# Two 4 MB loads in place of four 2 MB loads for each expert's gate-up weights

## The reference, cut to what matters

```
logits = t @ router_w + router_b                 # 1024 tokens, 32 experts
top_logit, top_idx = top_k(logits, 4); gates = softmax(top_logit)
for each expert e, for the tokens that chose it:
    gu   = t[tok] @ w_gate_up[e] + b_gate_up[e]  # (n, 1024) @ (1024, 2048), gate and up columns alternate
    gate = minimum(gu[:, 0::2], 7); up = clip(gu[:, 1::2], -7, 7)
    act  = (up + 1) * gate * sigmoid(1.702 * gate)
    y    = act @ w_down[e] + b_down[e]           # (n, 1024) @ (1024, 1024)
out[token] = x[token] + sum of gate * y over the token's 4 experts
```

## Time and profile before

| | us |
|---|---|
| median of 3 runs | 3649.79 |
| lowest and highest run | 3638.45, 3654.53 |
| the profiled execution's own time | 3661.44 |
| its span in the trace | 3659.8 |
| the stage of the experts in it | about 1490 to 3585 |
| the final sum over the experts in it | about 3585 to 3659 |

### The profile page before, as it was taken

The page is one execution under the profiler, slowest core; times in us unless marked ns, Lnnn a source line. Parts: engine busy times, 40 slices in busy tenths (PEclk is TensorE's granted clock), DMA queues, the critical chain, the costliest instruction groups (busy, mean ns, idle before and its releaser), DMA issues.

```text
span 3659.8 us, 46853 instructions
## 1 busy us (share of the span) xinstructions
PE 3127.2 (85%) x15932; PEld 2365.5 (65%) x15933; DVE 1224.1 (33%) x3422; ACT 601.5 (16%) x1419; POOL 182.9 (5%) x188
## 2 busy tenths in 40 slices
PE   3577747999995997599999999998999998999991
PEld 1344426777772564487777777786777786777770
DVE  1145541666662554222222222222222221222224
ACT  0011110545551332011000010000111010000110
POOL 0000000000000011100000000000000000000000
PEclk8788865999997996799999999999999999999995
DMA  3521133233004110665544576565776674645735
GB/s 116 171 50 49 38 74 83 57 78 78 13 1 139 35 41 18 251 237 203 185 165 165 197 265 208 190 233 194 259 257 219 205 244 164 223 152 183 262 124 236
DMA packets 306054, 554.51 MB, mean 152 GB/s; under 512 B 80350, under 2 KB 115422, under 8 KB 304840
## 3 DMA queue, kind: packets, MB, share of 16 engines
q1 hardware_dynamic: 265912, 509.39, 41.2%
q0 software_dynamic: 21152, 38.50, 3.1%
q10 hardware_dynamic: 18832, 4.33, 0.5%
HBM read 525.89 MB, written 70.93 MB: 163 GB/s over the span
## 4 chain that ended last, share of the span: by engine, by line
PE 51%; issue 3%; DVE 2%; DMA 2%; ACT 1%; DVEq 1%; ACTq 0%; POOL 0%; POOLq 0%
PE ps L1587 32%; PE ps L1598 18%; DMA d_ys<-ys_e,dst 1%; PE ps L1570 1%; DVE x L1557 1%; ACT xT_e L1486 1%; DVE ys_e L1546 0%; DVE gg L1533 0%; DVEq L1402 0%; DMA xg<-d_h,src 0%; DVEq L1399 0%; ACTq L1405 0%; ACTq L1500 0%; ACT ss L1505 0%; DVE aT L1540 0%
## 5 line engine op out<-in xcount | busy, mean ns | idle before, releaser
L1587 PE MATMUL ps<-xT_e,wg 128*128 128x128 f32 (+2 forms) x8192 | 1274.8, 320 | 77.2 <-issue 40.4
L1587 PEld LDWEIGHTS ps<-xT_e,wg 128*128 128x128 f32 x8192 | 1233.1, 202 | 132.7 <-issue 57.9
L1598 PE MATMUL ps<-wd,aT 128*128 128x512 f32 x1504 | 650.8, 592 | 0.0
L1598 PEld LDWEIGHTS ps<-wd,aT 128*128 128x128 f32 x1504 | 283.5, 190 | 344.1 <-issue 344.1
L1533 DVE TENSOR_SCALAR gg<-ps,bias 128x128 f32<-128x128 f32 (+2 forms) x256 | 101.5, 396 | 792.7 <-PE ps L1587 792.5
L1546 DVE COPY ys_e<-ps 128x1024 f32<-128x1024 f32 x47 | 56.1, 1221 | 670.9 <-PE ps L1598 670.9
L1505 ACT ACTIVATE ss<-gg 128x128 f32<-128x128 f32 (+2 forms) x256 | 88.7, 346 | 962.3 <-DVE gg L1533 962.0
L428 PE MATMUL ps<-w_in,hT_a 128*128 128x430 f32 x512 | 187.6, 529 | 0.0
L1505 ACT ACT_TABLE_LOAD x32 | 41.1, 1283 | 879.8 <-issue 879.8
L777 ACT ACTIVATE sc<-sc,nm 128x640 f32<-128x640 f32 (+15 forms) x256 | 161.3, 633 | 70.1 <-DVE nm L810 70.1
L428 PEld LDWEIGHTS ps<-w_in,hT_a 128*128 128x128 f32 x512 | 98.2, 193 | 87.4 <-issue 87.0
(11 more groups left out here) (284 smaller groups left out, 2505.6 us busy)
## 6 DMA issues: line engine op xcount, KB each, us to landing
wg<-in_w_gate_up SPq DMA_DIRECT2D x128, 2048.0 KB, 8.0
wd<-in_w_down SPq DMA_DIRECT2D x128, 1024.0 KB, 4.9
wg<-d_ys SPq DMA_DIRECT2D x8, 2048.0 KB, 10.8
d_bias<-d_rev SPq DMA_DIRECT2D x1, 10368.0 KB, 39.6
w_in<-in_w_in SPq DMA_DIRECT2D x1, 6880.0 KB
x_a<-in_x POOLq DMA_DIRECT2D x8, 512.0 KB, 8.4
kn<-d_kn SPq DMA_DIRECT2D x8, 512.0 KB
strip_t<-d_bias SPq DMA_DIRECT2D x8, 512.0 KB
```

Of the source, the lines that this page charges most:

```text
L1587: mm = pe.matmul(ps[:, j % 2, half * PASS:half * PASS + w], wg[:, j // 2, k, c0:c0 + 255:2], xT[:, k, 0:w], start=(k == 0), stop=(k == KD ...
L1598: mm = pe.matmul(ps[:, 2 + 2 * b + h, :], aT[:, j, b * P:(b + 1) * P], wd[:, c, j % 2, h * 512:(h + 1) * 512], start=(j == 0), stop=(j == ...
```

## The change

The same 8 MB per expert and pass are brought by two transfers of 4 MB. The buffer `wg` keeps its size, 64 KB in each partition, but is laid out as two halves of 1024 columns, so that each contiguous run of a transfer has 4 KB in place of 2 KB. PE waits for a half before groups 0 and 4, where it waited for a quarter before groups 0, 2, 4 and 6. SP may issue a half when four groups are done, where it could issue a quarter when two were. The final sum uses the same quarters of the buffer as before, addressed in the new layout. The down weights, the arithmetic and everything else stay.

```diff
-        wg = sb("wg", [P, NCH, KD, 512])
+        NCG = 2
+        wg = sb("wg", [P, NCG, KD, 1024])
...
-        s_wg = [sem(f"e_wg{c}") for c in range(NCH)]
+        s_wg = [sem(f"e_wg{c}") for c in range(NCG)]
...
-                        for c in range(NCH):
-                            sp.wait_ge(s_gu, CREDIT + JD * i + 2 * (c + 1) - JD)
+                        for c in range(NCG):
+                            sp.wait_ge(s_gu, CREDIT + JD * i + 4 * (c + 1) - JD)
                             hold(sp, e.sp_passed)
-                            sp.dma_start(wg[:, c, :, :], e.w_gate_up[0][one, :, c * 512:(c + 1) * 512].rearrange("o (k p) n -> p (o k) n", p=P)).then_inc(s_wg[c], 16)
+                            sp.dma_start(wg[:, c, :, :], e.w_gate_up[0][one, :, c * 1024:(c + 1) * 1024].rearrange("o (k p) n -> p (o k) n", p=P)).then_inc(s_wg[c], 16)
...
-                    sp.dma_start(wg[:, t % NCH, :, :].rearrange("p a b -> p (a b)"),
+                    sp.dma_start(wg[:, t % NCH // 2, 4 * (t % 2):4 * (t % 2) + 4, :].rearrange("p a b -> p (a b)"),
...
-                    yr = wg[:, t % NCH, :, :].rearrange("p (k c) n -> p k (c n)", k=TOPK)
+                    yr = wg[:, t % NCH // 2, 4 * (t % 2):4 * (t % 2) + 4, :]
...
-                                if j % 2 == 0:
-                                    pe.wait_ge(s_wg[j // 2], CREDIT + 16 * i + 16)
+                                if j % 4 == 0:
+                                    pe.wait_ge(s_wg[j // 4], CREDIT + 16 * i + 16)
...
-                                    c0 = 256 * (j % 2) + half
+                                    c0 = 256 * (j % 4) + half
...
-                                        mm = pe.matmul(ps[:, j % 2, half * PASS:half * PASS + w], wg[:, j // 2, k, c0:c0 + 255:2], xT[:, k, 0:w],
+                                        mm = pe.matmul(ps[:, j % 2, half * PASS:half * PASS + w], wg[:, j // 4, k, c0:c0 + 255:2], xT[:, k, 0:w],
```

## The result

The changed kernel takes 3693.56 us (median of 4 runs, 3689.94 to 3699.58) where the one before takes 3649.85. The ratio is 1.0126 with a 95% interval of 1.0099 to 1.0153. I had said 3658 and at most 3679: the change is slower by 43.7 us, more than five times the 8 us that I worked out. It is the case that I had listed as the unlikely slower rival.

What follows compares the result with a forecast made beforehand. The expert stage was taken as bound by PE, weight loads hidden. Late scatters behind small passes, +7.3 us, and the stage's start, +0.7, gave +8 us on the median 3649.79: 3658 us, range 3641 to 3679.

Steps and rivals of the forecast that it cites:

- unlikely slower rival: Ends of 13 small passes: scatter waits for backlog, up to 2.6 us each; +35 us, 3685; decides from 1.4; chance 0.15.
- The bound: Expert stage, 2095 us: PE is busy 95%, no wait names a weight load, so the rearranged transfers are already hidden.
- the issues on SP: SP queue: two loads and two issues fewer, 0.37 us per issue on an engine nobody waits for; gain nothing.
- the bigger runs: Gate-up loads: 4 KB runs at 407 instead of 389 GB/s save 32 us of DMA time under PE's work; gain nothing.
- the landings of the halves: Gate-up halves land later, 13 us after issue, but 18 to 19 us before needed in the tightest place; cost nothing.
- The place of the cost: End of small passes (width 128): 0.7 MB or 1.7 us of weight backlog delays the scatter; +7.3 us in sum.
- I take half of their spread, 0.7 us: Cost of one late scatter behind a small pass, from nine scatters of 2.85 to 4.23 us.
- my bounds of 0 and 2.6: One late scatter: nothing if its rows slip between load packets, 2.6 us if one whole down load goes ahead.
- The turns between queues: DMA queues before the scatter: it meets one packet of weights per turn, not the whole backlog; cost between 0 and 2.6 us.
- My own sign of being wrong: PE's waits for `aT` at the 7 small passes with width 128 next growing by over 1.4 us each.
- About 0.4 us where 192 follows: Six small passes followed by width 192: part of the scatter's delay is covered, about 0.4 us each, 2.4 us together.
- The start of the stage: First gather beside the first weights: longer runs delay its packets, 1.4 us at most; half taken, +0.7 us.

## Why the prediction was wrong

**The bound, the issues on SP, the bigger runs, the landings of the halves**: right. PE waits for no half, loads land after 12.9 us where I had 13, PE's busy time is unchanged, and in the versions without the scatter's chain the layout makes no difference that can be measured. One comparison in the prediction says less than it seems to: the 389 and 407 GB/s of rows 9 differ by the length of the runs. By the size of a transfer they go the other way, since the 407 are those of the 1 MB loads.

**The place of the cost**: right. The backlog in front of the scatter was the one cost found, the queues run full to the scatter as worked out (I had 1.7 us of work left over at the moment the down loads used to end), and the scatter, ACT, `aT`, group 2 are late in that order, at the 13 small passes that I counted and at none with 256 next.

**"I take half of their spread, 0.7 us"**: this is the step that failed. The cost of one late scatter was 2.05 us, nearly three times as much, and inside my bounds of 0 and 2.6. It is about the whole 1.7 us of the backlog and a little more. The value came from nine scatters whose spread isn't the price of this backlog: with the down loads held back the spread is gone (2.15 to 2.17 us), so it too came from the weights in front of each scatter. I had the backlog itself in hand, and it was the nearer number. The turns between queues, which stood beside this from the Trainium skill (DMA: Bandwidth & Descriptors, section "Queues, rings and completion order"), put the cost only somewhere between my two ends. What the runs show in its place is that the scatter moves no packet until the backlog is through, up to about 4 us after its issue: 1.5 to 1.7 us with no weights queued, 2.1 to 2.5 before, 3.9 to 4.3 after. In the chain's step at the boundary shown this is 2.16, 2.95 and 5.07 us, and 6.24 and 7.21 with 1 and 2 MB more. My own sign of being wrong, waits that grow by over 1.4 us each, came true.

**"About 0.4 us where 192 follows"**: wrong by the same step. The cover there was as good as used up, and the six places lost 2.2 us each. With 2.05 us at all 13 places the sum would have been 26.7 us, and the span grew by 28.5.

**The start of the stage**: 0.7 us forecast, and the gather's 8.16 us became 8.40.

**The chances**: 0.15 for the rival that came true, "it decides from 1.4 us per place on", was too little for a case whose price was worked out from rows and lay close to that point. In the time its forecast of 3685 is nearer to 3693.6 than mine.

**What stays open**: of the 43.7 us between the medians, more than even my upper bound of 35, the two traces show 28.5. The profiled execution before was 11.65 us above the median of its runs, and no other execution of it was traced, so I can't say which of its waits were longer than usual. One "issue" wait, behind the 15th pass, looks like a candidate, with 8.9 us in the trace before and about 3.3 in many others of these traces. But it is 9.0 in the changed kernel's trace as well, and 3.2 in that kernel's second trace, whose span of 3688.7 us is the same. So it doesn't explain the difference.

## What to carry to other kernels

Bulk loads that nobody waits for can still cost: ask what small transfer on the critical path is issued while they drain, and add up the bytes that stand in front of it at that moment. Where the DMA engines are near full there, making transfers larger and later moves bytes into that window, and if I can work out how long the backlog is, I take that as the price of whoever comes after it, up to the 4 us or so at which it flattened here. The remedies are to hold bulk loads with slack back until the small transfer has landed (0.7% here), and better, to let nobody wait for it (1.5%); both together gave 1.9 to 2.1%.

## What the runs showed of the hardware that I had not expected

A scatter issued from POOL moved no packet for 4 to 5 us while SP's queue was full of weight loads, and with 2 MB more queued it then shared the engines with them; with no weights queued the first packet came after 1.5 to 1.7 us, and the step in the chain took 2.16. The delay grew steeply with the first megabyte that was added and little with the second: PE's wait at the seven places with 128 next averages 2.84 us before, 6.10 with 1 MB more and 6.77 with 2 MB more.

PE pays more for such a wait than the wait itself. These are windows of the changed kernel right behind its 4.73 us wait (the last three columns are the granted clock, the DMA share and GB/s; the first pair is PE's busy time and its products):

```profile
2638.00:2643.00 5.00, 0.27 (x2) 0.27 (x2) 0.61 (x3) 1.62 (x3) 1.45 (x2) 0.85 0.09 10
2643.00:2646.00 3.00, 3.00 (x15) 3.00 (x16) 1.18 (x4) 0.28 (x1) 0.60 (x1) 0.50 0.36 114
2646.00:2649.00 3.00, 3.00 (x19) 3.00 (x19) 0.00 (x0) 0.00 (x0) 0.00 (x0) 0.62 0.00 0
2649.00:2652.00 3.00, 3.00 (x28) 3.00 (x27) 1.42 (x5) 0.31 (x1) 0.00 (x0) 1.00 0.00 0
```

The granted clock falls to 0.50 of full, 1.2 for 2.4 GHz, after the wait, and there are 15 products in 3 us where there are 28 at full clock. The kernel before has this after its shorter waits too (0.56 from 2631 to 2634, after the 2.60 us wait), which is why the change hardly added to it: the gate-up stretches of the 32 passes grew by 31.2 us in all, and 29.2 of these are the waits. Where ACT doesn't wait for the scatter, here in the kernel before with the late load of the target rows, the same stretch of a small pass runs through at full speed:

```profile
2637.56 30.31 PE L1587 MATMUL ps<-xT_e,wg 128*128 128x128 f32 x256
```

That is 30.31 us from the first to the last gate-up product, where the changed kernel takes 2668.09 - 2630.31 = 37.8 for the pass shown above: 4.73 are the wait, and some 2.7 more are mostly the clock. It explains why taking 37 us of waits out of the kernel before won 58 us in the medians, at least in part: added up in PE's timeline, the gate-up stretches of its 32 passes are 57 us shorter than before, 1254.5 for 1311.6, of which the waits are 37.
